# One combined gather of 8 KB rows against two gathers of 4 KB rows, in a decoder step with a product-key expert layer

## What is computed

```
q = rms_norm((x @ w_q).reshape(t, 8, 256), q_g).reshape(t, 8, 2, 128)
s = einsum('thcd,hcnd->thcn', q, sub_keys)          # two half keys of 128 each
s_top, i_top = top_k(s, 16)
cand = s_top[:, :, 0, :, None] + s_top[:, :, 1, None, :]
best, pos = top_k(cand, 16)                          # 16 experts of 16384 per head
idx = (i_top[...0] * 128 + i_top[...1]) at pos
g = softmax(best)
u = take(u_tab, idx); act = gelu(einsum('thkd,td->thk', u, x))
v = take(v_tab, idx)
f = einsum('thkd,thk->td', v, g * act)
y = layer_norm(ALPHA * x + f)
```

## Time and profile before

| | us |
|---|---|
| median of 3 runs | 3567.24 (3566.49 to 3580.76) |
| the profiled execution, its own time | 3567.98 |
| its span from first to last instruction | 3566.2 |

### The profile page before, as it was taken

One profiled execution on the slowest core, in us unless ns is written; L12 is line 12 of the kernel. 1 busy time (PEld: TensorE's weight loads), 2 busy tenths in 40 slices (PEclk: granted clock), 3 DMA queues, 4 the chain that ended last, 5 costly groups with the idle time before them and its releaser, 6 DMA issues.

```text
span 3566.2 us, 44522 instructions
## 1 busy us (share of the span) xinstructions
PE 2629.3 (74%) x14204; PEld 1100.5 (31%) x14204; DVE 2421.3 (68%) x5555; ACT 1511.4 (42%) x4361; POOL 1280.6 (36%) x1100
## 2 busy tenths in 40 slices
PE   8978788776677668756876677667767777677676
PEld 5646444331133113312331233123312232332211
DVE  8625745596569656976597659765976587445875
ACT  1114334344444443444343544454435444454443
POOL 0001234334443444344434443444344424223344
PEclk9988899886887688767887887788767877889866
DMA  5356899999999999999999999999999999999988
GB/s 158 86 173 241 319 336 421 394 376 418 421 381 377 420 421 379 375 421 421 380 374 417 421 382 388 414 421 377 394 397 421 381 406 383 405 405 368 390 345 336
DMA packets 246881, 1314.21 MB, mean 369 GB/s; under 512 B 50438, under 2 KB 74790, under 8 KB 96234
## 3 DMA queue, kind: packets, MB, share of 16 engines
q0 software_dynamic: 156672, 1140.92, 78.7%
q1 hardware_dynamic: 78368, 158.44, 12.2%
q10 hardware_dynamic: 11610, 12.01, 1.0%
HBM read 1291.70 MB, written 17.97 MB: 367 GB/s over the span
## 4 chain that ended last, share of the span: by engine, by line
DMA 29%; DVE 27%; PE 26%; ACT 7%; issue 7%; SPq 2%; POOL 1%; DVEq 0%; POOLq 0%; ACTq 0%
DMA UV<-in_peer_uv,zone_x 26%; DVE zone_z L1690 12%; PE psum L1338 9%; PE psum L1254 3%; PE psum L381 3%; PE psum L521 3%; PE psum L1279 2%; DMA wq<-in_cache_k 2%; DVE zone_x L1589 1%; DVE zone_x L1592 1%; DVE zone_x L1590 1%; POOL UV L1132 1%; ACT D L1451 1%; DVE zone_z L1651 1%; DVE zone_x L1591 1%
## 5 line engine op out<-in xcount | busy, mean ns | idle before, releaser
L1338 PE MATMUL psum<-UV,D 64*64 64x512 f32 x8704 | 1477.9, 771 | 847.7 <-ACT D L1451 822.4
L1132 POOL DMA_INDIRECT UV<-in_peer_uv,zone_x x1088 | 1275.0, 1172 | 2184.0 <-PE psum L1338 1820.5
L1690 DVE CUSTOM_DVE_ANT_0 zone_z<-UV,zone_x 128x1024 bf16<-128x1024 f32 x1088 | 1333.6, 1226 | 699.5 <-DMA UV<-in_peer_uv,zone_x 626.0
L1446 ACT ACTIVATE ge<-acts 128x1 f32<-128x1 f32 x1088 | 219.6, 202 | 1567.2 <-DVE acts L1690 1560.3
L1338 PEld LDWEIGHTS psum<-UV,D 64*64 64x64 f32 x8704 | 308.4, 157 | 1699.3 <-issue 1668.3
L1451 ACT ACTIVATE D<-id,wge 128x64 f32<-128x64 f32 x1088 | 378.4, 348 | 35.5
L1448 ACT ACTIVATE wge<-ge,zone_x 128x1 f32<-128x1 f32 x1088 | 320.5, 295 | 35.3
L1279 PE MATMUL psum<-wq,zone_z 128*128 128x256 f32 (+1 forms) x1152 | 308.4, 427 | 1.2 <-ACT zone_z L1389 1.2
L1279 PEld LDWEIGHTS psum<-wq,zone_z 128*128 128x128 f32 (+1 forms) x1152 | 236.6, 211 | 117.2 <-issue 68.1
L1446 ACT ACT_TABLE_LOAD x115 | 147.5, 1283 | 2.8 <-ACT vrows L651 0.8
L1254 PE MATMUL psum<-w_out_sb,zone_z 128*128 128x512 f32 (+1 forms) x256 | 116.6, 609 | 3.1 <-DMA w_out_sb<-in_w_out 3.1
(11 more groups left out here) (301 smaller groups left out, 2218.2 us busy)
## 6 DMA issues: line engine op xcount, KB each, us to landing
wq<-in_peer_w_q SPq DMA_DIRECT2D x72, 1024.0 KB, 9.4
UV<-in_peer_uv,zone_x POOLq DMA_INDIRECT x1088, 12.1
wq<-in_cache_k SPq DMA_DIRECT2D x64, 256.0 KB, 11.5
vrows<-in_cache_v SPq DMA_DIRECT2D x64, 256.0 KB
wq<-in_w_in SPq DMA_DIRECT2D x11, 1024.0 KB, 5.0
zone_x<-in_x_all SPq DMA_DIRECT2D x9, 512.0 KB, 8.2
UV<-in_w_out SPq DMA_DIRECT2D x2, 2048.0 KB, 12.0
w_out_sb<-in_w_out SPq DMA_DIRECT2D x1, 4096.0 KB, 33.2
```

Of the source, the lines that this page charges most:

```text
L1132: pool.indirect_dma_start(out=UV[:, n % RING, :], out_offset=None, in_=table, in_offset=bass.IndirectOffsetOnAxis(ap=icur[:, t % 2, column ...
L1338: ins = pe.matmul(bank[6 + r][q:q + 64, :], D[64 * r:64 * r + 64, n % RING, :], UV[64 * r:64 * r + 64, n % RING, DM + 512 * e:DM + 512 * e ...
L1446: act.activation(ge[:, j:j + 1], acts[:, j:j + 1], ACT.Gelu).then_inc(sem("gelu_done"), 1)
L1690: dve.tensor_tensor_reduce(out=junk[:, :], in0=UV[:, n % RING, 0:DM], in1=x1[:, t % 2, :], scale=1.0, scalar=0.0, op0=ALU.mult, op1=ALU.ad ...
```

## The change

The table is no longer joined: `peer_u` and `peer_v` stay two tables with rows of 4 KB, and each step issues two gathers of 128 x 4 KB with the same indices, v first. The same SBUF space that held seven slots of 8 KB holds eight v slots and six u slots. The v gather of step n waits for `vsum_done` of step n - 8, the u gather behind it for `dot_done` of step n - 6. The dot waits for the u slot, the matmuls for the v slot.

Three edits stand beside it. GLU block 1 goes from front position 20 of tile 0 to 7 on PE, to 15 on ACT and 19 on DVE (its store to 20), and uses banks 6 and 7. The wait for `h_out` leaves DVE's startup and stands at the first head's square on ACT and at the first `dve_combine`. The copy of transposed keys goes from DVE to ACT, behind the unit's own copy and store.

```
-RING = 7
+RING = 8
+URING = 6
-        UV = sb("UV", [P, RING, 2 * DM])
+        UV = sb("UV", [P, (RING + URING) // 2, 2 * DM])
...
+        vring = cut(uvf, 0, RING, DM)
+        uring = cut(uvf, RING * DM, URING, DM)
...
-            return ((3, 5) if n < 4 else (1, 3))[n % 4 // 2]
+            return ((3, 5) if n < 4 else (6, 7) if n < 8 else (1, 3))[n % 4 // 2]
...
-            dve.wait_ge(sem("h_out"), 64)
...
-        def dve_unit_columns(dve, i):
+        def act_unit_columns(act, i):
...
-            dve.wait_ge(sem("k_T"), 4 + i + 1)
-            dve.tensor_copy(kT[:, 2 * blk:2 * blk + 2, t * P:t * P + r],
+            act.wait_ge(sem("k_T"), 4 + i + 1)
+            act.activation(kT[:, 2 * blk:2 * blk + 2, t * P:t * P + r],
...
+            rows = bass.IndirectOffsetOnAxis(ap=icur[:, t % 2, column(t, k):column(t, k) + 1], axis=0)
             wait(pool, "vsum_done", n - RING + 1)
-            pool.indirect_dma_start(out=UV[:, n % RING, :], out_offset=None, in_=table,
-                                    in_offset=bass.IndirectOffsetOnAxis(ap=icur[:, t % 2, column(t, k):column(t, k) + 1], axis=0))\
-                .then_inc(sem(f"uv_in{n % RING}"), 16)
+            pool.indirect_dma_start(out=vring[:, n % RING, :], out_offset=None, in_=v_table, in_offset=rows)\
+                .then_inc(sem(f"v_in{n % RING}"), 16)
+            wait(pool, "dot_done", n - URING + 1)
+            pool.indirect_dma_start(out=uring[:, n % URING, :], out_offset=None, in_=u_table, in_offset=rows)\
+                .then_inc(sem(f"u_in{n % URING}"), 16)
...
+                if n == 0:
+                    wait(act, "h_out", 64)
                 wait(act, "q_ps", n + 1)
...
-            if t == 0 and f - 1 in GLU_AT:
-                act_glu(act, 1 + GLU_AT.index(f - 1))
+            if t == 0 and (f - 8 if f < base(0) + 20 else f - 1) in GLU_AT:
+                act_glu(act, 1 + GLU_AT.index(f - 8 if f < base(0) + 20 else f - 1))
...
+                if t == 0 and g == 0:
+                    wait(dve, "h_out", 64)
...
-            if t == 0 and f - 3 in GLU_AT:
+            if t == 0 and (f - 12 if f < base(0) + 25 else f - 3) in GLU_AT:
...
-        GLU_AT = [base(0) + 20, base(0) + 28, base(0) + 33, base(0) + 38]
+        GLU_AT = [base(0) + 7, base(0) + 28, base(0) + 33, base(0) + 38]
...
                             act_unit(act, i)
+                            if 1 <= i <= 14:
+                                act_unit_columns(act, i - 1)
...
-                        i = unit_at_step(t, k, 1)
-                        if i is not None and 1 <= i <= 14:
-                            dve_unit_columns(dve, i - 1)
```

More of the change, by code:

```diff
@@ L1035, in column, with u_landed, v_landed @@
             return k if t < NT else 2 * (k - k % TOP) + k % TOP
-        def landed(n):
-            return f"uv_in{n % RING}", 16 * (n // RING + 1)
+        def u_landed(n):
+            return f"u_in{n % URING}", 16 * (n // URING + 1)
+        def v_landed(n):
+            return f"v_in{n % RING}", 16 * (n // RING + 1)
         def sp_pages(sp, b, kind, half):
@@ L1332, in pe_expert @@
                 wait(pe, "sum_read", t)
-            pe.wait_ge(sem(landed(n)[0]), landed(n)[1])
+            pe.wait_ge(sem(v_landed(n)[0]), v_landed(n)[1])
             wait(pe, "diag_done", n + 1)
@@ L1434, in act_front @@
                 act_head(act, t, e, r)
-            if t == 0 and f - 1 in GLU_AT:
-                act_glu(act, 1 + GLU_AT.index(f - 1))
-            if t == 0 and f - 4 in GLU_AT:
-                act_glu_store(act, 1 + GLU_AT.index(f - 4))
+            if t == 0 and (f - 8 if f < base(0) + 20 else f - 1) in GLU_AT:
+                act_glu(act, 1 + GLU_AT.index(f - 8 if f < base(0) + 20 else f - 1))
+            if t == 0 and (f - 13 if f < base(0) + 25 else f - 4) in GLU_AT:
+                act_glu_store(act, 1 + GLU_AT.index(f - 13 if f < base(0) + 25 else f - 4))
             for g in range(3):
@@ L1679, in dve_front @@
                 dve_head(dve, step, t, e, r)
-            if t == 0 and f - 3 in GLU_AT:
-                dve_glu(dve, 1 + GLU_AT.index(f - 3))
+            if t == 0 and (f - 12 if f < base(0) + 25 else f - 3) in GLU_AT:
+                dve_glu(dve, 1 + GLU_AT.index(f - 12 if f < base(0) + 25 else f - 3))
             for g in range(3):
@@ L1687, in dve_expert @@
             n = number(t, k)
-            dve.wait_ge(sem(landed(n)[0]), landed(n)[1])
+            dve.wait_ge(sem(u_landed(n)[0]), u_landed(n)[1])
             wait(dve, "dot_done", n)
-            dve.tensor_tensor_reduce(out=junk[:, :], in0=UV[:, n % RING, 0:DM], in1=x1[:, t % 2, :], scale=1.0,
+            dve.tensor_tensor_reduce(out=junk[:, :], in0=uring[:, n % URING, :], in1=x1[:, t % 2, :], scale=1.0,
                                      scalar=0.0, op0=ALU.mult, op1=ALU.add, accum_out=acts[:, n % RING:n % RING + 1])\
@@ L1859 @@
 _INS = ["x_all", "x_T", "cache_k", "cache_v", "page_table", "w_in", "lambdas", "attn_subln_g", "ssm_prm", "ssm_d",
-        "ssm_w_glu", "ssm_b_glu", "w_out", "ln1_g", "ln1_b", "peer_w_q", "peer_q_g", "peer_keys", "peer_uv",
+        "ssm_w_glu", "ssm_b_glu", "w_out", "ln1_g", "ln1_b", "peer_w_q", "peer_q_g", "peer_keys", "peer_u", "peer_v",
         "ln2_g", "ln2_b"]
```

8 lines of the change are left out of this document (4 added, 4 removed).

## The result

The changed kernel takes **3792.9 us** (median of 4 runs, 3778.53 to 3794.6) against 3571.91 us before (4 runs beside it): a ratio of 1.061, with an interval of 1.057 to 1.064. The profiled execution has a span of 3792.8 us, 226.6 more than before.

The account below looks back on a forecast made before the run. DMA bytes were taken to bound the attention stretches, DVE and its chain the top-16 ones; after the change, POOL's issue. Span 3566.2 + 218 - 18.7 - 3.7 - 12 = 3749.8, stated as 3750 us, range 3570 to 3850.

Parts of the forecast that it names:

- Price of a gather: On POOL: a 4 KB gather takes the same issue time as an 8 KB one, mean 1.172 us plus 0.30 gap.
- rings pay: Rival: 4 KB issue is cheaper (0.47 us free), POOL never binds, top-16 stretches gain up to 53 us; 3520 to 3573, chance 0.11.
- Pace of the attention stretches: In the attention stretches POOL's two gathers set the pace: 2.95 us a step instead of 2.56, +218 us.
- held once per step: Rival: nearly each step has one gather held 0.61 us by a dot; 3.10 us a step, 3834 us, chance 0.17.
- In step: Rival: dots and gathers settle so that few are held, POOL does two per dot, bytes bind; 3573 us, chance 0.14.
- Packets of 4 KB: On the DMA queues: two 4 KB packets take 2.8% more than one of 8 KB; +39 us, hidden under POOL's time.
- Top-16 stretches: In stretches with top-16 work: 50 steps need POOL 148 us, which fit into 158, so nothing is added.
- Rings: Gather waits with six u and eight v slots: gain up to 53 us, loss up to 20, taken as 0.
- the wait for the states: At the serial start: moving the h_out wait lets the first map and the w_out projection start earlier, -18.7 us.
- The GLU term: Tile 0: GLU block 1 leaves the place between the first head's sums and its third top-16, -3.7 us.
- The key copies: Tile 0, 370 to 500 us: moving key copies from DVE to ACT gives -12 us (0 to -16), DMA binding next.

Follow-up runs that it names:

- the one gather with the same bytes: Kernel before with one gather of a 4 KB row per step, used for both the dot and the matmuls: 3186.6 us, ratio 0.892.
- two of 2 KB: Changed kernel with every gathered row cut to 2 KB, half the bytes in the same 2176 gathers: 3706.8 us, ratio 1.038.
- a sum of one input: Changed kernel with the dot replaced by a plain sum over the u row, x1 left out: 3755.4 us, ratio 1.051.
- the old slots: Kernel before with two gathers of 4 KB rows into halves of the same seven slots, old wait, no small edits: 3820.8 us, ratio 1.069.
- the kernel with the small edits: Kernel before with the three side edits alone, one gather of 8 KB rows per step as before: 3520.4 us, ratio 0.986.

## Why the prediction was right, and where it was not

The forecast was 3750 us, within 3570 to 3850; it came to 3792.9. The cause, POOL's issue of a second gather, is confirmed by the half bytes and by the one gather with the same bytes. Some signs were off: POOL is busy 2366 us and not 2550, the mean issue is 1.085 us where 1.1 to 1.3 was expected, and the DMA share is 0.95 and not 0.9.

*Price of a gather.* Right: median 0.94 us whatever the row (0.949 with 2 KB), gap 0.30. That the work is "per index" isn't shown: every gather of every run has 128 indices, and only the length of the rows was varied. The rival "rings pay" rested on a cheaper issue and is out.

*Pace of the attention stretches.* 2.95 forecast, 2.96 measured, but with another composition: the mean issue is 1.085 and not 1.172, which gives 2.77, and 0.19 us are waits, mostly for late releases. That the two errors cancel is luck. Where next to no release is late, in the attention stretches of two of 2 KB, the composition is the forecast one: a mean issue of 1.18 and 2.36 + 0.60 = 2.96 us. A timeline of after shows how a gather escapes or is held.

```profile
1651.43 0.94 POOL L1139 DMA_INDIRECT UV<-in_peer_v,zone_x  x1 [0.30 <-issue]
1651.62 1.23 DVE L1703 CUSTOM_DVE_ANT_0 zone_z<-UV,zone_x 128x1024 bf16<-128x1024 f32 x1 [1.30 <-DMA UV<-in_peer_u,zone_x]
1652.67 0.99 POOL L1142 DMA_INDIRECT UV<-in_peer_u,zone_x  x1 [0.30 <-issue]
...
1662.09 1.23 DVE L1703 CUSTOM_DVE_ANT_0 zone_z<-UV,zone_x 128x1024 bf16<-128x1024 f32 x1
1662.30 1.83 POOL L1139 DMA_INDIRECT UV<-in_peer_v,zone_x  x1 [0.30 <-issue]
```

The gather at 1651.43 started 0.19 us before the dot and ran through; the next started 0.18 before its end and lost 0.05. The one at 1662.30 started 0.21 after the dot and was held until 0.81 after its end. Only 32% of the gathers took over 1 us, fewer than the rival "held once per step" wants (50%); that rival's 2.48 + 0.61 didn't come. "In step" didn't either. The dots run a rhythm of 2.5 us for a moment (1649.09 and 1651.62), and then a v gather, at 1659.62, has waited 3.46 us for a late release. But late releases aren't all that stands against it: in the attention stretches of two of 2 KB next to nothing is lost to them, and 48% of the gathers take over 1 us.

The Trainium skill (SBUF — State Buffer, Who interferes with whom) has a VectorE instruction with two SBUF inputs contend with a GpSimd instruction that reads SBUF. The runs agree: with a sum of one input 4% of the gathers take over 1 us, and the mean falls to 0.95. It also reports a probe in which a `tensor_tensor` did not stall a GpSimd DMA. That doesn't hold for these gathers, even with a plain `tensor_tensor`, as long as both its inputs are in SBUF; one with an input in PSUM lets them through. From the trace of after:

```profile
794.37 1.49 DVE L1656 TENSOR_TENSOR zone_y<-zone_z,iot 128x1280 f32<-128x1280 f32 x1
794.62 2.06 POOL L1142 DMA_INDIRECT UV<-in_peer_u,zone_x  x1 [0.31 <-issue]
```

```profile
750.01 1.22 DVE L1551 TENSOR_TENSOR zone_x<-zone_x,psum 128x1024 f32<-128x1024 f32 x1
750.40 0.94 POOL L1142 DMA_INDIRECT UV<-in_peer_u,zone_x  x1 [0.30 <-issue]
```

The first gather ends 0.82 us after the operation, as it does after a dot; the second takes its 0.94.

*Packets of 4 KB.* The +2.8% doesn't hold for the gathers. It came from the 4 KB packets of another queue, 0.162 us each. By the packets in the trace, the gathers' own take 0.176 us on average (1610 to 1810) where one of 8 KB took 0.314 (before, 1520 to 1718): two take 12% more. That goes with a DMA share above the forecast. It isn't a fixed price either: with one gather of 4 KB rows a packet takes 0.200 us, at a DMA share of 0.76 (1350 to 1500).

*Top-16 stretches.* This step failed. They "fit into 158, so it stays as it is": on average POOL did fit (50 pairs in 160 us), yet the steps from 97 to 20 of the next tile, which are the top-16 stretches of the earlier trace rows, went from 3.18 to 3.29 us each, 33 us over six tiles (the whole rest, 3.10 to 3.23, 54 us). The average hides what happens inside. Before, steps 104 to 111 took 2.05 us each (mean of tiles 1 to 6), behind eight of 3.80. Two gathers of mean length need POOL 2.77 us, so it can't catch up like that: these steps take 2.98 after, 7 us more a tile, and the eight before them give back less than 2 (3.57). And the stretches did depend on bytes: 2.97 us a step with one gather of half the bytes. Bytes in 4 KB packets, holds (3.09 to 2.88 without them, at half the bytes) and late releases (208.2 us of idle time on ACT instead of 83.0) can each have a part, and how large it is isn't told apart. The packets' 39 us had been put under POOL's time in the attention stretches; that the other stretches could pay them had been left out.

*Rings.* Right, near 0: attention 2.96 and rest 3.21 with the old slots. The six u slots are enough; five aren't.

*Three small edits.* The first gather at 272 was forecast and came at 276.0. Of the -22.4 the wait for the states held (-18.7 forecast, -18.5 here):

```profile
232.04 7.13 PE L1263 MATMUL psum<-UV,zone_z 128*128 128x512 f32 x16 [0.79 <-DVE zone_z L1583]
...
250.20 1.22 DVE L1557 TENSOR_TENSOR zone_x<-zone_x,psum 128x1024 f32<-128x1024 f32 x1 [5.34 <-PE psum L1232]
```

The projection through `w_out` starts at 232.04; before it was 250.55. The GLU term (-3.7) is wrong: the norm's second addition waits 5.34 us for gains behind the GLU matmuls, a wait that the forecast had named as the price (+4.6) and then taken to be hidden. The key copies were worth -23 and not -12. The next bound was the DMA, as forecast, but its room was read from its share (0.88) and not from its rate: 324 GB/s against 405 in the row below is a room of a fifth, 26 us of 130. That the DMA is the bound there fits its share of 1.01, but PE is busy 140.6 of the 150 us too, and no run parts the two. From 350 to 500 us the kernel with the small edits issues 53 gathers, the kernel before 39:

```profile
350.00:500.00 150.00, 140.62 (x828) 81.75 (x827) 98.64 (x217) 70.81 (x224) 60.07 (x53) 0.98 1.01 405
```

In the changed kernel tile 0 shows none of it (432.5 us against 433.0). The copies do stand on ACT there, but the second gather takes back the 30 us. POOL isn't the only bound: from 360 to 480 its busy time and gaps make 108 of 120 us at a DMA share of 0.99, and with rows of 2 KB the tile takes 415.1 us.

*The sum.* By spans: small edits -44.4 (-34.4 forecast), second gather +271 on top of them (+218 forecast). Of the +271, 187 lie in the attention stretches of tiles 1 to 6 (177 forecast), 35 in their top-16 stretches (0 forecast), 29 in tile 0 (18 forecast) and 28 in the sample tile and the last tile (22 forecast), less some 9 at the ends. The second gather cost 53 us more than forecast and the small edits brought 10 more, so the misses partly cancel.

## What to carry to other kernels

With the same 128 indices, an indirect gather that isn't held costs its issuing engine the same, 0.94 us, whether its rows have 2, 4 or 8 KB. Before one is split, multiply the issues by their mean duration plus the gap, hold times included, and compare with the time of a step in every kind of stretch, and with its fast steps and not only its mean. A stretch in which the new cost is hidden by one bound still pays the other costs of the change: go through all stretches for each term. And a wait on a slot isn't a shortage of slots before the release and the work that gives it have been set side by side.

## What had not been expected of the hardware

- Signals of PE that arrive up to 18 us (by the next increment on record) after the records of the matmuls end, several of them within 0.3 us, in five of the six traces with two gathers a step. Where they occur, the trace also lacks some increments (996 of 1089 recorded in after, all in before). Whether PE, its signals or their recording is late is open; that other engines go on only then is shown by their idle times.
- Gathers of 2 KB, 4 KB and 8 KB rows take POOL 0.949, 0.940 and 0.941 us (medians). In the kernel with one gather of 4 KB rows 53% take over 1 us and the median is 1.050, the shortest 0.932. With 8 KB rows the attention stretches move 420 GB/s, with two gathers of 4 KB rows 356 at a DMA share of 0.95.
